# Out projections by chunks of 384 tokens, with the next projection's operands made during their last chunk

## The reference

```python
for i in range(DEPTH):                       # i = 0: Fourier mixer, i = 1: differential attention
    sh, sc, gt = adaln_params(cond, w_ada[i], b_ada[i])
    h = rms_norm(x, norm_g[i]) * (1.0 + sc) + sh
    o = mixer_i(h, w_in)                     # projections, mixer, gate: 2048 channels
    x = x + gt * (o @ w_out)                 # out projection, 2048 -> 1024
y = rms_norm(x, final_norm_g)
```

## Time and profile before

| | us |
|---|---|
| median of 3 runs (lowest to highest) | 2276.51 (2275.43 to 2277.13) |
| the profiled execution | 2275.64 |
| its span, first to last instruction | 2273.9 |
| PE busy | 2180.5 (96%) |
| DVE busy | 1143.3 (50%) |
| ACT busy | 785.7 (35%) |

### The profile page before, as it was taken

How to read it: one execution, slowest core, us unless ns; L and a number is a source line. 1 busy time by engine, 2 the same in 40 slices (tenths; PEclk the granted TensorE clock), 3 DMA queues, 4 the chain that set the end, 5 groups by cost and what they waited for, 6 DMA issues and landing times. The chain is left out here.

```text
span 2273.9 us, 33235 instructions
## 1 busy us (share of the span) xinstructions
PE 2180.5 (96%) x13671; PEld 2093.2 (92%) x13671; DVE 1143.3 (50%) x1646; ACT 785.7 (35%) x1357; POOL 88.6 (4%) x42
## 2 busy tenths in 40 slices
PE   7999999979997999999999999999999999989995
PEld 3999877979997999999999999989999999979995
DVE  4778464661227444544411132228888888874213
ACT  3511133141114111211221233336676666662111
POOL 0000000000000112211100000000000000000000
PEclk9999999989998999999999999999999999999997
DMA  8355343583214554666622544452444443215224
GB/s 326 135 172 182 125 150 120 211 322 103 88 46 187 142 151 125 184 151 155 164 79 89 210 166 168 144 189 104 158 158 158 158 158 144 104 60 192 88 69 188
DMA packets 104018, 342.20 MB, mean 150 GB/s; under 512 B 12512, under 2 KB 39264, under 8 KB 93664
## 3 DMA queue, kind: packets, MB, share of 16 engines
q1 hardware_dynamic: 103904, 340.60, 43.7%
HBM read 225.70 MB, written 114.82 MB: 150 GB/s over the span
## 5 line engine op out<-in xcount | busy, mean ns | idle before, releaser
L833 PE MATMUL p_ps<-p_h_hi,p_w_hi 128*128 128x384 f32 x1152 | 268.6, 336 | 9.1 <-DVE p_h_lo L1011 4.6
L833 PE MATMUL p_ps<-p_h_lo,p_w_hi 128*128 128x384 f32 x1152 | 268.1, 336 | 0.0
L833 PE MATMUL p_ps<-p_h_hi,p_w_lo 128*128 128x384 f32 x1152 | 267.9, 335 | 0.0
L833 PEld LDWEIGHTS p_ps<-p_h_hi,p_w_hi 128*128 128x128 f32 x1152 | 207.0, 189 | 10.0 <-issue 9.8
L833 PEld LDWEIGHTS p_ps<-p_h_hi,p_w_lo 128*128 128x128 f32 x1152 | 206.9, 189 | 0.0
L833 PEld LDWEIGHTS p_ps<-p_h_lo,p_w_hi 128*128 128x128 f32 x1152 | 206.9, 189 | 0.0
L1716 PE MATMUL o_ps<-o_y_hi,o_w_hi 128*128 128x384 f32 x768 | 176.6, 338 | 20.2 <-DVE o_w_lo L1764 16.8
L2050 ACT ACTIVATE a_e<-a_ps,a_nmax 128x1152 f32<-128x1152 f32 x127 | 155.4, 1224 | 62.8 <-DVE a_nmax L2111 62.8
L1716 PE MATMUL o_ps<-o_y_lo,o_w_hi 128*128 128x384 f32 x768 | 175.6, 336 | 0.0
L1716 PE MATMUL o_ps<-o_y_hi,o_w_lo 128*128 128x384 f32 x768 | 175.3, 336 | 0.0
L2007 PE MATMUL a_ps<-a_v_hi,a_at_hi 128*128 128x256 f32 x576 | 173.0, 300 | 0.0
(11 more groups left out here) (275 smaller groups left out, 4202.2 us busy)
## 6 DMA issues: line engine op xcount, KB each, us to landing
p_w_raw<-w_in_dram SPq DMA_DIRECT2D x32, 1024.0 KB, 6.6
g_wada<-w_ada_dram SPq DMA_DIRECT2D x16, 1024.0 KB, 6.7
f_w_raw<-w_u_dram SPq DMA_DIRECT2D x32, 512.0 KB, 4.2
o_w_raw<-w_out_dram SPq DMA_DIRECT2D x32, 512.0 KB, 4.1
g_dram<-g_stage SPq DMA_DIRECT2D x16, 576.0 KB, 3.2
f_g<-g_dram SPq DMA_DIRECT2D x8, 1152.0 KB, 7.8
y_dram<-f_y SPq DMA_DIRECT2D x8, 1152.0 KB, 5.4
x_dram<-o_x_new SPq DMA_DIRECT2D x16, 576.0 KB, 4.9
```

Source lines behind the costliest of these rows:

```text
L833: return pe.matmul(ps[:, 4 * b + c, 0:CH], a, x[:, c * CH:(c + 1) * CH], start=(d == 0 and j == 0), stop=(d == DT - 1 and j == 2))
```

## The change

`out_project` is turned round. All weights stay in SBUF (128 KB of each partition), and y passes through by chunks of 384 tokens: `y_hi` and `y_lo` hold one chunk. For chunks 0 and 1 PE goes over e outside and d inside, so that each weight row e is used as it comes; for chunk 2 over d outside, so that the tiles of x end one after another. y pieces of chunk 1 are split into the place of chunk 0 four rows behind it (`LAG`), once PE has used that place (`freed`). The load of the k-th y piece waits for `y_lo_done` of the piece four before it. The weights are reordered on the host from halves to rows e. y, x and their stores move in pieces of 192 KB; there are four y buffers. g and y of the mixers get places in SBUF that let the weights be written while the last stores of y are in flight.

`InverseRms` is cut in two: chunks 0 and 1 (`early`) are done by PE between the tiles d = 1 and 2, and d = 2 and 3, of the last chunk, and chunk 2 (`last`) afterwards. In layer 0, during the last chunk, chunks 0 and 1 of the new x are read back, normalised and split to h (`next_norm`, `next_hi`, `next_lo`), and the first weights of the attention projection are loaded and the first unit split; `project` starts with products on them and does chunk 2's part afterwards. In layer 1 chunks 0 and 1 of x are read back and normalised to y during the last chunk, chunk 2's tiles are normalised where they lie, from the factor in PSUM, and `final_norm` is gone. The POOL memset of `sh.ss` goes too.

```diff
 def out_project  @@ sync
+            for e in range(ET):
+                if e >= 2:
+                    sp.wait_ge(w_lo_done, e - 1)
+                    tiles.load_w(sp, w_src, e)
+                load_y(0, e)
+                if e >= LAG:
+                    load_y(1, e - LAG)
+                if e < 6:
+                    load_x(0, e)
...
+            for c in range(LAST):
+                for d in range(DT):
+                    sp.wait_ge(x_done, DT * c + d + 1)
+                    sp.dma_start(x_dst[d][:, chunk(c)], x[d]).then_inc(x_out[d], 16)
+                for d in range(DT):
+                    sp.wait_ge(x_out[d], 16 * (c + 1))
+                    sp.wait_ge(sq_done, DT * c + d + 1)
+                    load_x(c + 1, d)
...
+            if y_out is not None:
+                sp.wait_ge(tile_done, DT * LAST + 2)
+                for c in range(LAST):
+                    sp.dma_start(done_x[:, c], x_dst.rearrange("d p t -> p d t")[:, :, chunk(c)]).then_inc(again_in[c], 16)
+                for c in range(LAST):
+                    sp.wait_ge(normed, DT * (c + 1))
+                    sp.dma_start(y_out.rearrange("d p t -> p d t")[:, :, chunk(c)], done_x[:, c]).then_inc(y_stored, 16)
+                for d in range(DT):
+                    sp.wait_ge(normed, DT * LAST + d + 1)
+                    sp.dma_start(y_out[d][:, chunk(LAST)], x[d]).then_inc(y_stored, 16)
+                sp.wait_ge(y_stored, 16 * (LAST + DT))
+            else:
+                for d in range(DT):
+                    if d == 3:
+                        sp.wait_ge(tile_done, DT * LAST + 3)
+                        for c in range(LAST):
+                            following.load_x(sp, x_dst, c)
+                    if d == 6:
+                        sp.wait_ge(tile_done, DT * LAST + 6)
+                        for n in range(2):
+                            following.load_w(sp, n)
+                    sp.wait_ge(x_done, DT * LAST + d + 1)
+                    sp.dma_start(x_dst[d][:, chunk(LAST)], x[d]).then_inc(x_out[d], 16)
 @@ tensor
+            for c in range(LAST):
+                for e in range(ET):
+                    pe.wait_ge(y_lo_done, place[c, e] + 1)
+                    if c == 0:
+                        pe.wait_ge(w_lo_done, e + 1)
+                    for d in range(DT):
+                        if e == 0 and c > 0:
+                            pe.wait_ge(x_done, DT * (c - 1) + d + 1)
+                        mm = products(d, e)
...
+            for d in range(DT):
+                pe.wait_ge(x_done, DT * (LAST - 1) + d + 1)
+                if d >= 5:
+                    pe.wait_ge(early_rms.done, 2)
...
+                if d == 1:
...
+                    early_rms.sums(pe)
+                if d == 2:
+                    early_rms.turns(pe)
+            if y_out is not None:
+                pe.wait_ge(ss_done, DT * NCH)
+                last_rms.sums(pe)
+                last_rms.turns(pe)
 @@ scalar
+                if c > 0:
+                    freed(act, c - 1, e)
+                act.copy(y_hi[:, e, :], y_raw[:, k % NR, :]).then_inc(y_hi_done, 1)
...
+            for c in range(LAST):
+                for d in range(DT):
+                    square(c, d)
+                    if d == 0:
+                        y_hi_half(c + 1, ET - 1)
...
+            for d in range(DT):
+                square(LAST, d)
...
+                if following is not None and d in (5, 6):
+                    next_hi(d - 5)
+            if following is not None:
+                following.split_hi(act, 0, 1)
 @@ vector
+            for e in range(ET):
+                w_lo(e)
+                if e == 4:
+                    for semaphore, count in stored:
+                        dve.wait_ge(semaphore, count)
+                y_lo_half(0, e)
+                if e >= LAG:
+                    y_lo_half(1, e - LAG)
...
+            for c in range(LAST):
+                for d in range(DT):
+                    evict(c, d)
+                    if d == 1:
+                        y_lo_half(c + 1, ET - 1)
+                for d in range(DT):
+                    add(c, d)
...
+            for d in range(DT):
+                evict(LAST, d)
+                add(LAST, d)
+                if following is not None:
+                    if d in (4, 5):
+                        next_norm(d - 4)
+                    if d in (5, 6):
+                        next_lo(d - 5)
...
+                if y_out is not None and 3 <= d < DT - 1:
+                    for k in range(4 * (d - 3), 4 * (d - 2)):
...
+                        normalise(done_x[:, c, m, :], m, sh.ss[:, chunk(c)])
+            if following is not None:
+                following.split_lo(dve, 0, 1)
+            if y_out is not None:
+                last_rms.invert(dve)
+                dve.wait_ge(last_rms.spread, 1)
+                for d in range(DT):
+                    normalise(x[d], d, ps[:, 1, 0:CH])
 def project  @@ sync
-            sp.dma_start(w_raw[:, 0, :], w_src[0]).then_inc(raw_in[0], 16)
...
+            for semaphore in x_stored:
+                sp.wait_ge(semaphore, 16 * NCH)
+            tiles.load_x(sp, x_src, NCH - 1)
 @@ tensor
-            inverse_rms.tensor(pe)
+            inverse_rms.sums(pe)
...
                 for m, (c, d) in enumerate(STEPS):
+                    if m == 4:
+                        inverse_rms.turns(pe)
...
-            pe.wait_ge(inverse_rms.done, NCH)
 @@ vector
-            split_lo(0, 1)
-            for m in range(len(STEPS) + 1):
+            for m in range(2 * DT, len(STEPS) + 1):
```

More of the change, by code:

```diff
@@ L89, in tensor, with root @@
             if at == NCH - 1:
                 mm.then_inc(self.spread, 1)
-    def scalar(self, act, between=None):
+    def root(self, act):
         act.wait_ge(self.summed, 1)
-        act.activation(self.sh.rms[:, :], self.ps[:, 4, 0:TT], ACT.Sqrt, bias=self.sh.eps[:, 0:1],
+        act.activation(self.factor(), self.ps[:, self.sum_bank, self.first:self.stop], ACT.Sqrt, bias=self.sh.eps[:, 0:1],
                        scale=1.0 / D).then_inc(self.rooted, 1)
[L96 to L100, removed]
@@ L102, in vector, with copies, invert @@
-    def vector(self, dve):
+    def copies(self, act):
+        for k, bank in enumerate(self.banks):
+            c = self.first // NCH + k
+            act.wait_ge(self.spread, k + 1)
+            act.copy(self.sh.ss[:, c * CH:(c + 1) * CH], self.ps[:, bank, 0:CH]).then_inc(self.done, 1)
+    def invert(self, dve):
         dve.wait_ge(self.rooted, 1)
-        dve.reciprocal(self.sh.rms[:, :], self.sh.rms[:, :]).then_inc(self.inverted, 1)
+        dve.reciprocal(self.factor(), self.factor()).then_inc(self.inverted, 1)
@@ L582, in _, with project @@
             pool.memset(sh.eps[:, :], EPS).then_inc(ones_set, 1)
-def project(nc, sh, layer, x_src, w_src, kinds, rope, out, past=None, ahead=None, heads=None):
+def project(nc, sh, layer, tiles, x_src, x_stored, w_src, kinds, rope, out, past=None, ahead=None, heads=None):
     with ExitStack() as ctx:
@@ L632, in project @@
         ps = ctx.enter_context(nc.psum_tensor(f"p{layer}_ps", [P, 8, BANK], F32))
[L633 to L636, removed]
+        x, x_in = tiles.x, [sh.own(semaphore) for semaphore in tiles.x_in]
         PIECES = [[(slice(0, CH), 0)], [(slice(CH, 2 * CH), 0)], [(slice(2 * CH, NS), 0), (slice(NS, T), 1)]]
         STEPS = [(c, d) for c in range(NCH) for d in range(DT)]
[L641 to L644, removed]
+        t_done, h_hi_done, h_lo_done = (sh.own(semaphore) for semaphore in (tiles.t_done, tiles.h_hi_done, tiles.h_lo_done))
+        inverse_rms = InverseRms(sh, sem, ps, "last", 2 * NCH, TT, 3, (7,))
+        for semaphore in x_stored:
+            sh.own(semaphore)
         table_in = sem("table_in")
-        raw_in = [sem(f"raw_in{s}") for s in range(2)]
-        hi_ready = [sem(f"hi_ready{s}") for s in range(2)]
-        lo_ready = [sem(f"lo_ready{s}") for s in range(2)]
+        raw_in, hi_ready, lo_ready = ([sh.own(semaphore) for semaphore in pair]
+                                      for pair in (tiles.raw_in, tiles.hi_ready, tiles.lo_ready))
         proj_done = sem("proj_done")
@@ L1802, in final_norm @@
[L1802 to L1815 removed]
+        early_rms = InverseRms(sh, sem, ps, "early", 0, 2 * NCH, 6, (5, 7))
@@ L1816, in final_norm, with chunk @@
+        def chunk(c):
+            return slice(c * CH, (c + 1) * CH)
         block = ctx.enter_context(nc.Block())
```

464 lines of the change are left out of this document (237 added, 227 removed).

## The result

The kernel after takes 2243.45 us (median of 4 runs, 2242.72 to 2243.68), the kernel before in the same batch 2275.97 (2274.81 to 2277.13): a ratio of 0.9854, interval 0.9842 to 0.9867, 32.5 us or 1.5% faster. The forecast was 2250.5, its range 2244 to 2265. The direction is right; the size is 7 us short, and the time lies 0.6 us outside the range. The profiled execution took 2243.55 us with a span of 2241.7, 32.2 less than before's 2273.9.

What follows compares the result with a forecast made beforehand. PE, busy 96% of the span, was taken to bound the kernel. Terms -1.4 - 3.5 + 2.4 + 4.1 - 9.5 - 18.1 = -26.0 us gave a span of 2247.9, forecast 2250.5 us against the median; range 2244 to 2265.

Steps and rivals of the forecast that it cites:

- What bounds the kernel: PE, busy 96% of the span; its products stay the same in number, so time can come only from the edges.
- the four borders: Places the diff touches, at the front and behind each of the two out projections, where time was to be won.
- T0 to unit 1: From PE's last product of the first out projection (T0) to project's unit 1: -9.5 us (-7 to -11).
- Fronts: Start of both out projections: PE's first product 3.0 us behind ACT, 0.7 less than before, twice: -1.4 us.
- Inside the out projections: Three terms within both out projections, -3.5 + 2.4 + 4.1 us, from chunk 0, the change of chunks and the early factor.
- the waits of chunk 0: PE's waits of 2.5 and 1.0 us while chunk 0 fills would go: -3.5 us (0 to -3.5).
- the change of chunks: From chunk 0 to 1, DVE's evictions 2 to 7 start late: 1.2 us per stage, +2.4 (0 to +4.2).
- the early factor: Sums and transposes for chunks 0 and 1 inside PE's last-chunk stream: 2.05 us per stage, +4.1 (+2 to +8.2).
- The doubt on small transfers: In chunk 0, a step's four loads one after another would take 10.6 us, over 150 us worse; the prediction rejected this.
- The gap behind unit 0: PE's pause in project between units 0 and 1: DVE's drain alone, 2.6 + 0.4 us.
- The slow clock in front: First 4.8 us of project's products behind the first out projection again slow, +2.2 us.
- Tail: From PE's last product of the second out projection (T1) to the end: 14.2 against 32.3 us, -18.1 (-13.1 to -18.5).

Runs made afterwards that it cites:

- after_evict_first: Kernel after, with y_lo of (c + 1, 15) moved behind all eight evictions of the chunk in DVE's list: 2242.34 us, ratio 0.9854.
- after_no_prework: Kernel after, with project loading its first weights and all of x itself and doing all 24 steps, as before: 2252.91 us, ratio 0.9905.
- before_wait_moved: Kernel before, with SP's wait for the last two stores of x1 moved from out_project's end to project's reading of x: 2275.02 us, ratio 0.9998.
- after_late_split: Kernel after, with DVE splitting unit 1's weights only behind unit 0's last product: 2251.18 us, ratio 0.9884.
- after_old_tail: Kernel after, with final_norm again a stage of its own that loads x back by 8 tiles of 576 KB: 2258.26 us, ratio 0.9924.
- again: Kernel after run once more unchanged, as a control: 2242.67 us, ratio 0.985.
- one weight buffer: Kernel after, with the load of weight row e waiting for the split of row e - 1 instead of e - 2: 2291.63 us, ratio 1.0063.
- both last edits: after_evict_first, 2242.34 us; and on top of it, project's first weights split ahead of the last eight early norms, 2244.5 us.
- chunks only: Kernel after, with project's early operands and the new tail both undone; chunked out projections, early factor and small stores stay: 2268.23 us, ratio 0.9969.

## Why the prediction was right, and where it fell short

**What bounds the kernel** and the four borders were right: the sum over the stretches accounts for the whole change within 0.1 us. Of it, 1.7 us lie ahead of the four borders, where the forecast had nothing: 1.0 is chance, 0.7 the handovers. One of the four, T0 to unit 1, was mis-sized beyond its bounds.

**Fronts**: PE 2.8 us after ACT, forecast 3.0. ACT's and DVE's chains ran as described. The 0.7 us at the handovers into the out projections was not in the forecast, and it belongs to the change: from DVE's last work to ACT's first split it takes 1.16 and 1.21 us in the kernel before and its edit (three profiles) and 0.81 to 0.85 in all nine of after and its edits. In the kernel before, ACT first counts up five semaphores at the head of the stage (from 2034.4 to 2034.7 in layer 1); in after nothing stands between the barrier and the split. Instructions of these lines in the kernel before, both out projections: number, length in ns, first and last start.

```profile
L1725 ACTq EVENT_SEMAPHORE  x4: 17/17/17, 469.8 to 2034.5; - x4
L1728 ACTq EVENT_SEMAPHORE  x2: 17/17/17, 470.1 to 2034.7; - x2
```

**Inside the out projections**: forecast +3.0, measured +2.9, with the parts near their values: the waits of chunk 0 gone, one wait per stage at the change of chunks (0.7, on PE's weight loads 1.1; forecast 1.2), and the early factor's 12 sums in 1.4 us and six transposes in 0.8 in PE's stream (forecast 2.05). That the change of chunks is DVE's order was shown by `after_evict_first`. The doubt on small transfers was rightly decided. DMA issues in 479 to 500 us: number, KB each, median us to landing.

```profile
o_w_raw<-w_out_dram SPq DMA_DIRECT2D x7, 512.0 KB, 3.9
o_y_raw<-y_dram SPq DMA_DIRECT2D x14, 192.0 KB, 4.1
```

PE had no wait in steps of 4.16 us. The rule of the Trainium skill (DMA: Bandwidth & Descriptors, section Bandwidth) to batch to 1 MiB does not bind here: the trace disagrees, with 286 GB/s in 479 to 500 us from pieces of 192 and 512 KB, several in flight. The transfers of a step were not done one after another, which by the prediction's estimate would have taken 10.6 us. That section of the Trainium skill gives its figures for transfers issued from GpSimd; these are issued by SP.

**T0 to unit 1** is the step that failed, by its size: forecast -9.5, bounds -7 to -11, measured -13.1. The mechanism was right (the operands of chunks 0 and 1 made under PE's last chunk, as `after_no_prework` shows with 9.7 us); the pieces behind T0 were mis-sized, all in one direction:
- "The barrier takes 1.05 as now." It takes 0.32. The 1.05 had SP's wait for the landing of the last 576 KB store in it, as `before_wait_moved` showed. After, the store is 192 KB and lands in 1.8 us, long before DVE has split the weights. 0.7 us.
- "So the last eviction starts between T0 and T0 + 0.5; I take the latter." It starts at T0 + 0.03, at the other end: 0.5 us.
- "The gap behind unit 0 is the drain alone, 2.6 + 0.4". The gap is 2.28: 0.7 us.
- The slow clock behind the gap was left as before in the -9.5. It stayed at 2.4 GHz: 1.5 us. The text named this as a possible 1.4 more, and its best case of -10.9 is just -9.5 with that 1.4. So the bound held the clock, and nothing for the three others, which are 1.9 together. `after_late_split` shows that gap and clock go together: 3.0 us more of gap brought 2.3 of clock.

The slow clock in front, 4.8 us of products forecast, held until 689.3 with products from 684.5, and was rightly priced.

**Tail**: 13.8 against 14.2, and `after_old_tail` returns 15.6 us of it. That the number is so close is in part luck, since two errors cancel. The multiplications start at T1 + 4.0 instead of 5.3 and the last store leaves 1.5 us earlier than forecast: the three transposes took 0.54 instead of 1.0 and the sums 0.83 instead of 1.3, since the clock hadn't fallen; at the lower one they took about the forecast's times in `after_evict_first`. The store then lands in 1.8 us, not 3.2. Against these 2.9 us, the end behind the landing takes 3.7 us instead of the 1.2 carried over from the kernel before, because of the 47 clears. Nothing follows them; what leaving them out would bring was not tried.

**The range** took all bounds at their best for its lower end, -32.3 us, and that is by chance what the span measured, -32.2: inside the out projections it came out 4.4 worse than the best case, while T0 to unit 1 lay 2.2 beyond its bound, the fronts 0.4, and 1.7 came from ahead. The 0.6 us by which the median lies outside is about the 0.5 by which this batch's median of the kernel before lies under the 2276.51 that the range was counted from.

## What to carry to other kernels

- The time at a barrier belongs to whatever came last into it. Before one carries it over as a constant, look for a store whose landing an engine awaits at its end: 0.75 of 1.05 us was that.
- A gap of PE has two prices, its length and the clock behind it. Shortening one from 4.6 to 2.3 us won 2.3 and another 1.5; lengthening one by 3.0 lost 3.0 and another 2.3. A bound on such a gap has to hold both, and what is carried over as a constant besides.
- Where two engines' lists are full up to the end of a stage, moving work ahead in them wins nothing, and a wait that is really removed (1.0 us in each out projection here) may not show in a total that scatters by 4 us. Judge it by PE's stretch, in several profiles.
- When a stage becomes the last one, look at what its closing does behind the last store. Here it is 3.3 of the 13.8 us of tail, in instructions that the busy times of the page don't count.

## What the runs showed that was not expected

TensorE's clock behind a short pause isn't the same each time. After a pause of 2.28 us ahead of unit 1 it was kept in all six profiles that have it (after, again, one weight buffer, the old tail, and both last edits), and after 4.4 to 5.3 us it was lost in all six others (before twice, its edit, without early operands, chunks only, late split). But the pause of 1.98 us behind T1 was answered both ways. So was the one ahead of `attention`, 2.86 us in every profile: the clock was kept in nine and lost in three, and 3 us of `attention`'s 508 hang on it, up to 4 with a second such place near its end. What decides it was not found. Also by chance, it seems, PE's first product of the whole kernel starts between 6.3 and 7.2 us, whichever kernel runs.
